# A decoder step on one core: the prompt's attention scores from keys stacked as high and low part

## What is computed

```python
z = jnp.einsum('bqhd,bkhd->bhqk', qblk, k).astype(jnp.float32) * scale + bias_f
mask = k_pos[None, :] < pos[:, None]
log_keep = jnp.where(mask, jax.nn.log_sigmoid(-z), 0.0)
later = lax.cumsum(log_keep, axis=3, reverse=True) - log_keep
a = jnp.where(mask, jnp.exp(jax.nn.log_sigmoid(z) + later), 0.0)
return jnp.einsum('bhqk,bkhd->bqhd', a.astype(v.dtype), v)
```

## Time and profile before

| | us |
|---|---|
| median of 3 runs | 896.42 |
| lowest and highest run | 892.65, 899.86 |
| span of the profiled execution | 892.8 |
| PE busy in it | 851.5 (95%) |
| DVE, ACT, POOL busy in it | 554.1, 457.8, 278.7 |

### The profile page before, as it was taken

The page is one execution under the profiler, slowest core; times in us unless marked ns, Lnnn a source line. Parts: engine busy times, 40 slices in busy tenths (PEclk is TensorE's granted clock), DMA queues, the critical chain, the costliest instruction groups (busy, mean ns, idle before and its releaser), DMA issues.

```text
span 892.8 us, 14909 instructions
## 1 busy us (share of the span) xinstructions
PE 851.5 (95%) x5101; PEld 593.3 (66%) x5101; DVE 554.1 (62%) x676; ACT 457.8 (51%) x1534; POOL 278.7 (31%) x149
## 2 busy tenths in 40 slices
PE   5999999999999999999999999999989999999995
PEld 3566667767754444454478878878754544899995
DVE  4545475789856869979995722222267777555553
ACT  4612383236658677769673412212278676444433
POOL 3000000865766998995871000000100000021110
PEclk9999999999999999999999999999999999999998
DMA  9799868645599998988995079998898879321202
GB/s 329 267 370 392 314 228 294 218 156 211 193 314 365 368 336 297 333 327 329 349 349 198 1 253 342 353 326 294 299 330 297 314 273 364 99 96 48 95 1 97
DMA packets 109436, 232.53 MB, mean 260 GB/s; under 512 B 7473, under 2 KB 66552, under 8 KB 109360
## 3 DMA queue, kind: packets, MB, share of 16 engines
q1 hardware_dynamic: 50992, 172.16, 53.0%
q10 hardware_dynamic: 58368, 59.41, 20.0%
HBM read 220.41 MB, written 11.14 MB: 259 GB/s over the span
## 4 chain that ended last, share of the span: by engine, by line
PE 74%; DVE 10%; DMA 6%; ACT 5%; issue 3%; POOL 1%; SPq 1%; ACTq 0%; POOLq 0%; DVEq 0%
PE pp L1638 19%; PE pp L1625 14%; PE pp L1641 10%; PE pp L2059 6%; PE pp L2016 4%; DVE slot L1296 2%; PE pp L2043 2%; PE pp L1602 2%; DMA w_raw<-in_gla_w_in_dram 2%; PE pp L2030 2%; PE pp L1622 2%; PE pp L1653 2%; DVE w_lo L1112 1%; DMA slot<-in_cache_k_dram 1%; PE pp L1720 1%
## 5 line engine op out<-in xcount | busy, mean ns | idle before, releaser
L619 POOL TENSOR_TENSOR slot<-slot,qb 128x1024 f32<-128x1024 f32 x95 | 247.5, 2635 | 104.0 <-DMA slot<-in_cache_k_dram 66.0
L1297 DVE TENSOR_REDUCE zall<-slot 128x16 f32<-128x1024 f32 x99 | 119.1, 1215 | 19.1 <-POOL slot L619 17.9
L1112 DVE TENSOR_TENSOR w_lo<-w_raw,w_hi 128x1024 fp32r<-128x1024 f32 x57 | 81.8, 1436 | 75.3 <-ACT w_hi L669 75.3
L825 ACT ACTIVATE slot<-slot 128x64 f32<-128x64 f32 x464 | 111.0, 241 | 24.4 <-POOL slot L619 24.4
L669 ACT CAST w_hi<-w_raw 128x1024 fp32r<-128x1024 f32 x58 | 60.5, 1045 | 79.9 <-PE pp L1641 39.4
L825 ACT ACTIVATION_READ_ACCUMULATOR slot<-slot 128x1 f32 x464 | 86.7, 187 | 0.0
L1625 PE MATMUL pp<-xn,w_raw 128*128 128x512 f32 x192 | 84.3, 593 | 0.5 <-ACT xn L680 0.5
L1625 PE MATMUL pp<-xn,w_unsplit 128*128 128x512 f32 x192 | 83.9, 592 | 0.0
L1641 PE MATMUL pp<-xa_hi,w_hi 128*128 128x512 f32 x200 | 81.7, 408 | 1.6 <-DVE w_lo L1112 1.6
L1638 PE MATMUL pp<-xb_hi,w_hi 128*128 128x260 f32 x384 | 78.9, 287 | 1.1 <-DVE w_lo L1112 0.9
L1641 PE MATMUL pp<-xa_hi,w_lo 128*128 128x512 f32 x200 | 79.0, 395 | 0.0
(11 more groups left out here) (314 smaller groups left out, 1498.6 us busy)
## 6 DMA issues: line engine op xcount, KB each, us to landing
slot<-in_cache_k_dram SPq DMA_DIRECT2D x128, 512.0 KB, 5.7
slot<-in_cache_v_dram SPq DMA_DIRECT2D x120, 512.0 KB, 5.7
w_raw<-in_gla_w_in_dram ACTq DMA_DIRECT2D x12, 1024.0 KB, 8.9
slot<-in_gla_w_in_dram SPq DMA_DIRECT2D x24, 512.0 KB, 10.1
w_raw<-in_w_kv_dram ACTq DMA_DIRECT2D x8, 1024.0 KB, 10.2
w_raw<-in_w_ple_gate_dram ACTq DMA_DIRECT2D x6, 1024.0 KB, 5.3
s<-in_state_gla_dram SPq DMA_DIRECT2D x1, 4096.0 KB, 26.9
out_dram<-s ACTq DMA_DIRECT2D x4, 1024.0 KB, 11.1
```

The costliest lines, as they stand in the source:

```text
L619: nc.gpsimd.tensor_tensor(slot[s][:], slot[s][:], qb[:, (n // NPG) % 2, :], ALU.mult).then_inc(S("k_mul_pool"), 1)
L825: ins = nc.scalar.activation(part, part, ACT.Copy, accum_out=zall[:, n % NPG, b * SH + h:b * SH + h + 1])
L1112: nc.vector.tensor_tensor(lo, raw, hi.bitcast(F32), ALU.subtract).then_inc(S("w_split"), 1)
L1297: nc.vector.tensor_reduce(zall[:, n % NPG, b * SH:(b + 1) * SH], at.rearrange("p (h d) -> p h d", d=HD), AX.X, ALU.add).then_inc(S("k_used ...
```

## The change

- `K1T` is gone. Each head has its own stack of 128 rows (`kstack`): in the head's own 64 rows the high part of its keys (fp32r), in the other 64 rows the low part of the same keys. The stacks of heads 0 to 7 lie where `K1T` lay, those of heads 8 to 15 over `hT`.
- K tiles are written to `work` like V tiles. Per K tile, ACT makes the high parts in two copies (`high_keys`, after `kv_tile`), DVE the low parts in two subtractions (`low_keys`).
- The queries are split too. `q_hi` holds the high part in both halves of the rows, for each head. ACT writes the head's own half; for the first two pairs it writes the other half as well, and for pairs 2 to 7 two DMAs on the SP queue copy it there, issued ahead of the page loads of quads 19, 20, 22, 24, 26 and 28. `q_lo` (over `q1T`) is a subtraction on POOL, two a pair; the zero fills are gone.
- A block of scores is now two fp32r products: `q_hi` by the whole stack over 128 rows, and `q_lo` by the high keys over the head's 64 rows. The mask's matmul stays.
- `hT` is stored to DRAM in step 1 of the 24-step loop (ACT queue) and read back by the SP queue after the last scores, ahead of `pin1`. DVE waits for it before the first tile of `wo1`.
- Some semaphores are merged (`w2r_in` into `w2_in`, `p1_in` into `p_in`), so the first product with `w2` waits for all five loads.

```diff
-            for i in range(4):
-                pool.wait_ge(S("mm"), last_tile("V") - (1 if i < 2 else 0))
-                nc.gpsimd.memset(qz[i][HD:P, 0, :], 0.0)
-                nc.gpsimd.memset(qz[i][0:HD, 1, :], 0.0).then_inc(S("qz_zero"), 1)
+            for i in range(KT):
+                pool.wait_ge(S("q_hi"), i + 1)
+                for h in (2 * i, 2 * i + 1):
+                    r = head_rows(h)
+                    last = nc.gpsimd.tensor_tensor(q_lo[r, i, :], q1T[r, i, :], q_hi[i % 4][r, h % 2, :].bitcast(F32), ALU.subtract)
+                last.then_inc(S("q_lo"), 1)
...
+DOUBLED_AT = {19: 2, 20: 3, 22: 4, 24: 5, 26: 6, 28: 7}
...
+                if n % QUAD == 0 and quad in DOUBLED_AT:
+                    i = DOUBLED_AT[quad]
+                    sp.wait_ge(S("q_hi"), i + 1)
+                    sp.wait_ge(S("q_row"), 16 * GH + 32 * (i - 2))
+                    for h in (2 * i, 2 * i + 1):
+                        sp.dma_start(q_hi[i % 4][other_rows(h), h % 2, :].bitcast(F32), q_hi[i % 4][head_rows(h), h % 2, :].bitcast(F32)).then_inc(S("q_row"), 16)
                 load_page(n)
             sp.wait_ge(S("z_p"), len(ZBANKS) * SH)
-            sp.dma_start(pin1[:, :, :], p_prompt[1, 0].rearrange("(b p) d -> p b d", p=P)).then_inc(S("p1_in"), 16)
+            sp.dma_start(hT[:, :, :].rearrange("p k t -> p (k t)"), h_rows[:, :]).then_inc(S("h_moved"), 16)
+            sp.dma_start(pin1[:, :, :], p_prompt[1, 0].rearrange("(b p) d -> p b d", p=P)).then_inc(S("p_in"), 16)
...
-                nc.scalar.copy(qz[i % 4][0:HD, 0, :], q1T[0:HD, i, :])
-                nc.scalar.copy(qz[i % 4][HD:P, 1, :], q1T[HD:P, i, :]).then_inc(S("qz"), 1)
+                for h in (2 * i, 2 * i + 1):
+                    r = head_rows(h)
+                    last = nc.scalar.copy(q_hi[i % 4][r, h % 2, :], q1T[r, i, :])
+                    if i < 2:
+                        last = nc.scalar.copy(q_hi[i % 4][other_rows(h), h % 2, :], q1T[r, i, :])
+                last.then_inc(S("q_hi"), 1)
+
+            def high_keys(u):
+                act.wait_ge(S("evac"), PHASES["K"][2] + u + 1)
+                if u == KT // 2:
+                    act.wait_ge(S("h_moved"), 16)
+                for h in (2 * u, 2 * u + 1):
+                    last = nc.scalar.copy(stacked_keys(h)[head_rows(h), :], work[head_rows(h), 2 + u % 2, 0:NP_TOK])
+                last.then_inc(S("k_hi"), 1)
...
+                    if i == 1:
+                        act.dma_start(h_rows[:, :], hT[:, :, :].rearrange("p k t -> p (k t)")).then_inc(S("h_moved"), 16)
...
+            def low_keys(u):
+                dve.wait_ge(S("k_hi"), u + 1)
+                for h in (2 * u, 2 * u + 1):
+                    r = head_rows(h)
+                    last = nc.vector.tensor_tensor(stacked_keys(h)[other_rows(h), :], work[r, 2 + u % 2, 0:NP_TOK],
+                                                   stacked_keys(h)[r, :].bitcast(F32), ALU.subtract)
+                last.then_inc(S("k_lo"), 1)
...
-                pe.wait_ge(S("qz"), i + 1)
-                pe.wait_ge(S("qz_zero"), min(i + 1, 4))
+                    pe.wait_ge(S("k_lo"), KT)
+                pe.wait_ge(S("q_hi"), i + 1)
+                pe.wait_ge(S("q_lo"), i + 1)
+                if i >= 2:
+                    pe.wait_ge(S("q_row"), 16 * GH + 32 * (i - 1))
...
-                        last = nc.tensor.matmul(bank[bk][:, c0:c0 + n], qz[i % 4][:, h % 2, q * P:(q + 1) * P],
-                                                K1T[:, i, 0:n], start=False, stop=True, skip_group_check=True)
+                        r, qs = head_rows(h), slice(q * P, (q + 1) * P)
+                        nc.tensor.matmul(bank[bk][:, c0:c0 + n], q_hi[i % 4][:, h % 2, qs], stacked_keys(h)[:, 0:n],
+                                         start=False, stop=False, skip_group_check=True)
+                        last = nc.tensor.matmul(bank[bk][:, c0:c0 + n], q_lo[r, i, qs], stacked_keys(h)[r, 0:n],
+                                                start=False, stop=True, skip_group_check=True)
```

More of the change, by code:

```diff
@@ L237, in new @@
             return t
+        off_h = top[0]
         hT = new("hT", [P, KT, T])
@@ L332, in build @@
         q1T = new("q1T", [P, KT, NP_TOK])
-        K1T = new("K1T", [P, KT, T])
-        assert top[0] <= off_phase
+        q_lo = at("q_lo", [P, KT, NP_TOK], F32R, offA)
+        kstack = [new("kstack0", [P, KT, NP_TOK], F32R), at("kstack1", [P, KT, NP_TOK], F32R, off_h)]
+        assert top[0] <= off_phase and size([P, KT, NP_TOK]) <= size([P, KT, T])
         top[0] = offB + 2 * size([P, KT, T])
@@ L365, in build @@
         assert 6 * pz <= 2 * size([P, KT, T])
-        qz = [at(f"qz{i}", [P, 2, NP_TOK], F32, off_split + (0, 2, 1, 3)[i] * 4096) for i in range(4)]
+        q_hi = [at(f"q_hi{i}", [P, 2, NP_TOK], F32R, off_split + (0, 2, 1, 3)[i] * 4096) for i in range(4)]
         w_unsplit = [w_raw[:, 0, :], w_raw[:, 1, :]] + [at(f"w_unsplit{i}", [P, 2048], F32, off_split + i * 8192)[:] for i in range(2)]
         q_rows = nc.dram_tensor("q_rows", (NS, D), F32).ap()
+        h_rows = nc.dram_tensor("h_rows", (P, KT * T), F32).ap()
         pp = [ctx.enter_context(nc.psum_tensor(f"pp{i}", [P, 2, 512], F32)) for i in range(4)]
@@ L446, in x_gain, with head_rows, other_rows, stacked_keys @@
             return gcol[:, c:c + 1]
+        def head_rows(h):
+            return slice(h % 2 * HD, (h % 2 + 1) * HD)
+        def other_rows(h):
+            return head_rows(h + 1)
+        def stacked_keys(h):
+            return kstack[h // KT][:, h % KT, :]
         def last_tile(name):
@@ L542, in _ @@
                     sp.dma_start(w_up0[:, :, :], w_ple_up[0].rearrange("(k p) n -> p k n", p=P)).then_inc(S("up_in"), 16)
+                quad = (n - NPAGES) // QUAD
+                if n % QUAD == 0 and quad in DOUBLED_AT:
[4 more added lines that the diff above has]
+                        sp.dma_start(q_hi[i % 4][other_rows(h), h % 2, :].bitcast(F32), q_hi[i % 4][head_rows(h), h % 2, :].bitcast(F32)).then_inc(S("q_row"), 16)
                 load_page(n)
             sp.wait_ge(S("z_p"), len(ZBANKS) * SH)
-            sp.dma_start(pin1[:, :, :], p_prompt[1, 0].rearrange("(b p) d -> p b d", p=P)).then_inc(S("p1_in"), 16)
-            sp.dma_start(ps1[:, :], p_sample[1, :, 0, :]).then_inc(S("p1_in"), 16)
+            sp.dma_start(hT[:, :, :].rearrange("p k t -> p (k t)"), h_rows[:, :]).then_inc(S("h_moved"), 16)
+            sp.dma_start(pin1[:, :, :], p_prompt[1, 0].rearrange("(b p) d -> p b d", p=P)).then_inc(S("p_in"), 16)
+            sp.dma_start(ps1[:, :], p_sample[1, :, 0, :]).then_inc(S("p_in"), 16)
             for b in range(TB - 1):
@@ L1024, in _ @@
                     kv_tile(i - KV_LAG - 8)
+                if 8 <= i < 16:
+                    high_keys(i - 8)
             for t in range(16 - KV_LAG, 16):
@@ L1460, in _ @@
                     nc.vector.tensor_tensor(g1T[:, u, :], g1T[:, u, :], work[:, 2 + u % 2, :], ALU.mult).then_inc(S("silu"), 1)
-                elif i < 16:
-                    normed(j, K1T[:, u, :])
-                else:
-                    if u >= 2:
-                        dve.wait_ge(S("kv_t"), 8 + u - 1)
+                else:
+                    if i >= 10:
+                        dve.wait_ge(S("kv_t"), i - 9)
                     normed(j, work[:, 2 + u % 2, :])
+                    if i < 16:
+                        low_keys(u)
                 if done is not None:
@@ L1530, in _ @@
                 x_lo(5 * KT + i, g1T[:, i, :])
+            dve.wait_ge(S("h_moved"), 32)
             for u in range(8):
@@ L1761, in _ @@
             pe.wait_ge(S("s_lrt"), 1)
[L1762 removed]
+            pe.wait_ge(S("w2_in"), 16 * (1 + GH))
             for h in range(GH):
@@ L1976, in kv_transposes @@
                     pe.wait_ge(S("kv_out"), t)
-                token_major(K1T[:, t, :] if t < 8 else work[:, 2 + t % 2, :], S("kv_t"))
+                token_major(work[:, 2 + t % 2, :], S("kv_t"))
             def sample_scores_back(g):
```

7 lines of the change are left out of this document (3 added, 4 removed).

## The result

The changed kernel takes 906.09 us (median; 905.19 to 906.75) beside 894.79 for the kernel before: a ratio of 1.011, interval 1.008 to 1.015. I had predicted 892.2 and a range up to 901. Its profiled span is 903.5, 10.7 more than before.

A forecast was written before the change was run, and what follows sets the result against it. PE and ACT were taken to reach each step's end together, so little of PE's saving counts. Gains of 4.7 us less 0.5 for the restore give 4.2; 896.4 - 4.2 = 892.2, range 885 to 901.

The forecast's parts named there:

- The price of a pair of products: A head's scores on PE: 1.29 us instead of 2.33, 1.04 less, the 64-row low product priced by its columns.
- rival C: Scores: products after different row counts expose weight loads; 4.9 us in nine steps, start loses 1.3, about 902.6; chance 0.07.
- turning point: First group of scores: the sign turns to a loss once the pair of 256 columns costs more than 0.49 us.
- ACT's path: Loop steps: ACT needs 4.54 us without waiting, so steps 10 and 11 gain only 0.50 us each.
- Rival A: Whole stage: PE alone bounds and ACT follows; 16.6 us less, 879.8; chance 0.08.
- The start: First scores, steps 0 and 1: extra query copies add 1.3 us, net 0.2 more; step 1 gains 0.17.
- POOL's pair 0: Ahead of the first scores: POOL's two subtractions follow ACT's copies; bounds 0 to 1 us, taken as nothing.
- The K stage: K tiles: two ACT copies and two DVE subtractions a tile, about 1.3 us on each, hidden by PE.
- Restore, doublings, store, merged waits: Restore of hT before pin1: 0.5 us taken, bounds 0 and 7.4; the other three taken as nothing.
- D: End of the stage: restore of hT at 156 GB/s, 2.7 us more, 899.1; chance 0.13.
- E: Stage: DMA becomes the bound; pages late by 4 us at the end give 896; chance 0.10.
- B: Scores: 128-column products run at the f32 price of 0.25 us; gain falls to 2.0 us, 894.4; chance 0.17.

The follow-up runs named there:

- e1: Changed kernel with the low product over all 128 rows instead of the head's 64: 897.82 us, ratio 1.003 to the kernel before.
- e3: Changed kernel with the low product over 128 rows and pair 1's query copies moved right behind pair 0's: 893.94 us, ratio 0.999 to the kernel before.
- e7: Changed kernel with each bank group's high products all first, then its low ones: 904.29 us, ratio 1.011 to the kernel before.
- e9: Kernel before, with POOL also doing two unused 64x512 query subtractions for each pair of heads: 899.06 us, ratio 1.004 to the kernel before.
- e2: Changed kernel with pair 1's four query copies on ACT moved right behind pair 0's: 906.49 us, ratio 1.015 to the kernel before.
- e11: Best later version (full rows, earlier pair 1 queries, later low_keys(7), low queries of pairs 2 to 7 on DVE) with 64-row low product restored: 903.17 us, ratio 1.008.

## Why the prediction was wrong

- **The price of a pair of products.** This is the term that failed, in every step of the loop. I wrote of the low product over 64 rows "I take the price of its columns", with bounds of nothing and double. A product cost 0.145 us more than with equal rows (e1), eight times a head, as long as rows alternate. I had the mechanism as rival C, with 0.07, at 4.9 us over nine steps and 902.6 in all; the trace has about 0.28 us in each of twelve steps and 0.39 at the first scores, 3.8 together, where I had forecast a gain. Its turning point, a pair of 256 columns above 0.49, was wrong: that pair costs 0.48, and the step is longer all the same, through the second group (1.12 for 0.93). I gave it little because equal rows hid their loads; that says nothing about unequal ones.
- **ACT's path.** Right. In the changed kernel it passes the late second group on: ACT's run is 0.28 us longer, and so is the step. Once the products are cheap it gives the forecast times: 12.91 and 13.17 us a pair in e1 for 12.8 and 13.13, masks and scores 1.69 for 1.62 (1.29, and 0.33 of masks from the earlier trace rows). Rival A (PE alone) is out by the same rows: e1 takes 1.16 us of PE's work off a head, and the even step shrinks by 0.73 only.
- **The start.** This failed too, and by itself cost more: 5.8 of the 11.46 us. For the first scores and step 0 I forecast a net 0.2; with cheap products (e1) it was 0.85 less and 1.24 more, so 0.4. Step 1 was to gain 0.17 and lost 4.46. I had followed POOL's pair 0 only, and costed it as a delay of its own. POOL's subtractions for pairs 1 and 2 lie beside DVE's scans and products of head 1, where PE waits for DVE. I costed POOL's instructions, not what they do to DVE.
- **The clock.** I had taken it as 1.00, as before. It cost some 1.6 us in step 13, and 2.8 in step 1, which the 5.8 above include. With both causes mended (e3) the stage is 5.4 us shorter than before, where I had forecast 4.7; since e3 still loses time to POOL, a page and the clock, that agreement is in part luck.
- **The K stage.** "The only thing behind the waiting `low_keys` is the next `split_lo`" was wrong: behind the last one stand the samples' rows, for 0.8 us.
- **Restore, doublings, store, merged waits.** For the restore and the doublings nothing was the right size; I had 0.5 for the restore. The store and the merged waits lie ahead of the first value quad, which begins at 514.0 us for 515.4 before; that is within the scatter, and no run prices them. From the embedding's first transpose to the end it takes 126.3 us as before. The restore was issued at 764.74, landed 9.8 us later, and PE reached `pin1` at 777.16. Rivals D and E are out for this kernel: PE waits for neither `pin1` nor, in the stage, for a page. E has a grain of truth for the faster versions, which wait for pages. B is out too: a pair of 128 columns in e1 takes 0.26 us (725.26 to 725.52), not 0.50.

## What to carry to other kernels

A price read from products of one shape holds for a row of that shape. Here, where neighbouring products used different row counts, most of a weight load came out (0.145 of 0.19 us), and reading all rows, or grouping by shape, was cheaper than computing less. Before work goes to an idle engine, look at what runs beside it: POOL's two subtractions took 2.85 us of its own and 2.2 from DVE's products. And an edit that makes the bounding engine faster shows its worth only if the next one in the chain (here ACT, then the pages) has room, so read both from the same two steps.

## What was not expected of the hardware

- Where 64-row and 128-row products alternate, each of the eight costs 0.145 us more on average than where all have 128 rows, with the same columns; two changes of row count fewer give back 0.30 us (e7).
- In e1 two fp32r products of 128 columns over 128 rows take 0.13 us each (725.26 to 725.52), of 512 columns 0.31 and 0.23 (725.96 to 726.50).
- Two subtractions of 64x512 on POOL (2.85 us together) stretch DVE's four products from 1.70 to 3.87 us and three scans from 2.39 to 3.03, in the kernel before as well (e9).
- In the stage, the granted clock fell to 0.50 for 3 us and more with PE recorded as busy ahead of it in three of the five profiles whose row counts alternate within a head's scores (changed kernel, e2, e11), and in none of the other eight.
